# A two-block fp32 network on one core: attentions and scan rearranged, heads by pairs on halves of the array

## The chip, the cores and the metric

The kernel runs on one core of a Trainium2 chip. The metric is the device time of one execution in microseconds (us); the time before is the median of three runs, 975.42 us (974.31 to 978.83). Engines: PE is TensorE (matmuls), DVE is VectorE, ACT is ScalarE, POOL is GpSimd, SP issues the weight transfers.

## The reference

One sequence of 256 rows with D = 1024 goes through two blocks, all in fp32. What the change touches:

```
h = rmsnorm(x);  aq, ak, av, hq, hf_fwd, hf_bwd, hi, hg = split(h @ w_in)
att = attention(rope(norm(aq)), rope(norm(ak)), av)   # 8 heads of 64, 2 kv heads
rec = gated scan over the sequence, both directions, 4 heads of 128
x += rmsnorm(concat(att, rec) @ w_out)
m = rmsnorm(mem);  k, v = split(m @ w_xkv)
x += rmsnorm(attention(rmsnorm(x) @ w_xq, k, v) @ w_xo)   # 4 heads of 256
x += rmsnorm(conv_ffn(rmsnorm(x), w_up, w_down))          # D_FF 2816
# second block
oa = differential attention (8 heads, two maps of 64 each), subnormed
ob = latent attention (8 heads, 128 + 64 wide, block-causal)
x += rms_norm((sig(ga) * (oa @ w_proj_a) + sig(gb) * (ob @ w_proj_b)) @ w_o)
x += rms_norm(gated ffn)
```

## The kernel before, in words

**Products.** Each fp32 product is made of three fp32r products: high x high, low x high, high x low (`products`, L545). Weights stream through `sb_ring`, two slots of 2 MB, in the order of `chunks`; each chunk is cut into pieces of 128x1024. For each piece ACT copies the high half (`ahead`, L1420, `whi`) and DVE subtracts it for the low half (L1944, `wlo`); four lows, those of `xkv2`, are made by POOL (`POOL_LO`, `split_lo`). A piece's halves live in one of three homes or, for the long streams, in lent buffers (`lent1` to `lent9`). `ahead(m)` on ACT and DVE means: make all halves up to piece m now; `ahead_of(name, n)`: up to the n-th piece of a chunk; `reached[...]` holds how far PE has come at a step.

**Order.** Every engine's order is the written order of its block; the engines meet in semaphores. PSUM banks 0 to 3 serve the streamed products (`next_g`), 4 to 7 (`M`) the attentions, turns and sums; `Banks` pairs "filled" with "emptied". `gemm_rows` makes 128-row outputs, `cols_half` transposed ones, `row_pass` one row block over two chunks of 512 columns.

**Scan.** `next_level(n)` on DVE: `ahead`, `double_keys(n-1)` (L2083), `double_queries(n-1)` (L2093), `keep_level(n)` (L2068, copies masked scores out of the banks). PE's scores of a level are L742. `rope1(r)` (L2138 to L2152) stands between levels on DVE: it turns row block r of q and k, then scales it by the rstd that POOL makes (L1289).

**Attention** (`attend` on PE, ACT and DVE). At step n: scores of head n into bank 4 or 5 (PE L853 for the first attention, 64 rows of the array, by head in the upper or the lower half); turning of the probs of head n-1 into bank 6 (L817); values of head n-2 into bank 7 (L841; 64 columns of the array for the first attention); then a fill, a piece or two of another product. DVE: recip and scaling of the probs of head n-1 (L2195, L2199), then max of head n (L2215), lows, then taking the values of n-2 (L1982, L1983). ACT: exp of head n (L1590), highs, copy of the turned probs of n-1 (L1606). The second attention (`attx`) has no fill. In the third (`mla`) a piece of `w_proj_a` is the fill, and `normalise_oa(1)` and `take_v(1)` are DVE's.

**Around.** `mem_norm_g` is turned by `turn_norm` (L692): matmuls with a diagonal of rstd as the moving side. `w_xo` comes in two chunks of 512 columns, each over all rows, through `row_pass`; `into_ffn` on ACT and DVE squares each half row as it fills (L1647, L2281), adds it (L2289), and makes the tiles of the next norm (L1665, L2307), which PE turned (`turn_norm_rows`, L642). In `ffn`, DVE and ACT make the gate's and the value's taps (L2394, L1744) between lows. ACT's order at the end of the third attention: two highs of `w_proj_b`, sigmoids of the gates (L1878), with highs between.

```
attend, DVE:  probs(n-1); max(n); ahead(+1); fill; take(n-2); ahead(+2)
attend, ACT:  exp(n);  ahead(+1); copy turned(n-1); fill;     ahead(+2)
```

Of the kernel before, what the change touches and what calls it, by code (L numbers as in the profile page):

```python
# [36 lines left out]
P = 128  # L37
S = 256
# [116 lines left out]
def build(nc, a, out):  # L155
    ctx = ExitStack()
    with ctx:
# [246 lines left out]
        for n in ("w_out", "w_xq", "w_xo"):  # L404
            for i in range(2):
                chunk(f"{n}{i}", a[n], KT, 512 * i, 512)
            if n == "w_out":
                chunk("xkv3", a["w_xkv"], KT, 512 * 3, 512)
# [39 lines left out]
        for name, _, k, n in chunks:  # L448
# [9 lines left out]
            elif name == "ukv":  # L458
                w = w.rearrange("p k (h d) -> p k h d", d=2 * P)
                for part in (0, P):  # L460
                    for i in range(2):
                        piece(name, w[:, :, 4 * i:4 * i + 4, part:part + P])
            else:
                step_k = PIECE // n
                for k0 in range(0, k, step_k):
                    piece(name, w[:, k0:min(k0 + step_k, k), :], k0)
# [42 lines left out]
        POOL_LO = ("xkv2",)  # L509
        lo_there, lo_counts = [], {"lo_dve": 0, "lo_pool": 0}  # L510
        for name, _, _ in pieces:
            which = "lo_pool" if name in POOL_LO else "lo_dve"
            lo_counts[which] += 1
            lo_there.append((which, lo_counts[which]))

        def lo_done(m):

            return s(lo_there[m][0]), lo_there[m][1]
# [16 lines left out]
        def _(pe):  # L535
# [47 lines left out]
            def gemm_rows(name, T, part=None, readers=1):  # L583
# [6 lines left out]
                for q in range(lo, end):  # L590
                    m, w = next_piece(name)
                    k0 = pieces[m][2]
                    if q == 0:
                        for key in keys:
                            banks.take(pe, key, next_g(), readers)
# [38 lines left out]

            def turn_rows(name, src, r, half, b, ready, readers):
# [22 lines left out]
            def cols_half(name, T, half, readers=1):  # L658

                key = f"{name}.{half}"  # L660
                for j in range(2):
                    m, w = next_piece(name)
                    if j == 0:
                        banks.take(pe, key, next_g(), readers)
# [30 lines left out]

            turn_norm("pre_mix_g", x)
# [5 lines left out]
            turn_norm("mem_norm_g", mem)  # L702
# [83 lines left out]
            def by_rows(scores, spans):  # L786

                def both(u, os):
                    for r in range(R):
                        mm = scores(u, os[0][:, r * S:r * S + spans[r]], r, spans[r])  # L790
                    return [mm]
                return both

            def attend(name, units, ready, scores, values, spans, fill=(), v_every=1, at_once=1):

                turned = [u for u in range(units) if (u + 1) % v_every == 0]
                for step in range(units + 2):
                    if step < units and step % at_once == 0:  # L800
                        if step == 0:
                            ready()
                        keys = [f"{name}.s{u}" for u in range(step, step + at_once)]
                        for u, key in enumerate(keys, step):
                            banks.take(pe, key, M[u % 2], R)
                        done = scores(step, [bank[banks.at[key][0]] for key in keys])
                        for key, mm in zip(keys, done):
                            mm.then_inc(banks.fill(key), 1)
                    if step >= 1 and step - 1 in turned:
                        u = step - 1  # L810
                        pe.wait_ge(s(f"{name}_probs"), turned.index(u) + 1)
# [9 lines left out]
                    if step >= 2 and step - 2 in turned:  # L821
                        u = step - 2
                        n = turned.index(u)
# [3 lines left out]
                        mm = values(u, bank[M[3]], probsT[:, n % 2, :])  # L827
                        mm.then_inc(banks.fill(key), 1)
                    if step < len(fill):
                        f, args = fill[step]  # L830
                        f(*args)
# [18 lines left out]
            def scores1(h, o, r, n):  # L850
                lo = (h % 2) * ATT_DIM
                kv = h // (ATT_HEADS // ATT_KV)
# [1805 lines left out]
```

## Time and profile before

| what | us |
|---|---|
| median of the runs | 975.42 |
| the profiled execution | 976.41 |
| its span | 974.6 |
| PE busy | 917.2 |
| DVE busy | 619.5 |
| ACT busy | 479.6 |
| POOL busy | 87.1 |
| granted clock, mean | 0.989 |

The span is the profiled time less what lies around it (1.8 us). PE is the engine with the most work; its idle time and the stretches in which its granted clock is below 1 are what the order can change.

### The profile page before, as it was taken

The numbers are of one execution on the slowest core, as the hardware profiler recorded it, in microseconds if no ns is written. First come the engines' busy times: TensorE is split into PE (matmuls) and PEld (weight loads), VectorE is DVE, ScalarE is ACT, GpSimd is POOL, SyncE is SP. The second block draws the span as 40 slices with busy tenths as digits, with TensorE's granted clock in tenths as the row PEclk, the third lists the DMA queues.
The fourth block names the chain that finished last, engine by engine and source line by source line (L and its number), as shares of the span: only waits on it lengthen the run. The fifth ranks groups of instructions, "written<-read, shape, count | busy, mean of one in ns | idle before, by whom it ended". The sixth has DMA issues, their size and how long they took to land.

```text
span 974.6 us, 13972 instructions
## 1 busy us (share of the span) xinstructions
PE 917.2 (94%) x5556; PEld 804.0 (82%) x5556; DVE 619.5 (64%) x973; ACT 479.6 (49%) x841; POOL 87.1 (9%) x122
## 2 busy tenths in 40 slices
PE   6999699799989999999999999999898999999997
PEld 5988597479867999989978878788676879999996
DVE  4767774556457857576876666667677684363654
ACT  5844244455436735454553446666445562342541
POOL 1210103000002000000013310002003010000000
PEclk9999799999999999999999999999999999999999
DMA  9434232254335634645543645434225584346451
GB/s 328 175 130 158 82 107 88 85 173 159 123 98 183 217 130 158 217 145 182 207 152 118 217 173 173 135 136 174 87 87 182 163 284 170 130 160 227 135 172 43
DMA packets 92720, 152.56 MB, mean 157 GB/s; under 512 B 1968, under 2 KB 52272, under 8 KB 92400
## 3 DMA queue, kind: packets, MB, share of 16 engines
q1 hardware_dynamic: 92256, 150.94, 45.0%
q8 instruction: 44, 0.72, 0.3%
q10 hardware_dynamic: 288, 0.47, 0.2%
q0 software_dynamic: 112, 0.26, 0.1%
q14 instruction: 20, 0.16, 0.1%
HBM read 150.61 MB, written 1.05 MB: 156 GB/s over the span
## 4 chain that ended last, share of the span: by engine, by line
PE 67%; DVE 13%; ACT 5%; issue 4%; DMA 1%; DVEq 0%; ACTq 0%; POOLq 0%; POOL 0%
PE ps L545 58%; DVE sb_wlo L1944 2%; PE ps L841 2%; ACT sb_whi L1420 2%; DVE sb_b L2394 1%; PE ps L817 1%; DMA sb_ring<-in_w_in 1%; DVE sb_probs L2199 1%; PE ps L642 1%; DVE lent9lo L1944 1%; PE ps L678 1%; DVE lent8lo L1944 1%; PE ps L1060 1%; ACT lent8hi L1420 1%; ACT sb_b L1744 0%
## 5 line engine op out<-in xcount | busy, mean ns | idle before, releaser
L1944 DVE TENSOR_TENSOR sb_wlo<-sb_ring,sb_whi 128x1024 fp32r<-128x1024 f32 (+2 forms) x165 | 196.9, 1212 | 134.6 <-ACT sb_whi L1420 133.9
L1420 ACT ACTIVATE sb_whi<-sb_ring 128x1024 fp32r<-128x1024 f32 (+2 forms) x169 | 172.2, 1041 | 104.6 <-PE ps L545 98.2
L545 PE MATMUL ps<-sb_whi,sb_tbhi 128*128 128x512 f32 (+2 forms) x296 | 116.4, 393 | 3.8 <-DVE sb_wlo L1944 2.3
L545 PE MATMUL ps<-sb_whi,sb_tblo 128*128 128x512 f32 (+2 forms) x296 | 113.4, 383 | 0.0
L545 PE MATMUL ps<-sb_wlo,sb_tbhi 128*128 128x512 f32 (+2 forms) x296 | 113.3, 383 | 0.0
L545 PE MATMUL ps<-sb_whi,sb_tahi 128*128 128x512 f32 (+1 forms) x180 | 70.5, 391 | 9.3 <-DVE sb_wlo L1944 9.0
L545 PEld LDWEIGHTS ps<-sb_whi,sb_tbhi 128*128 128x128 f32 x296 | 55.6, 188 | 16.1 <-DVE sb_wlo L1944 3.6
L545 PE MATMUL ps<-sb_wlo,sb_tahi 128*128 128x512 f32 (+1 forms) x180 | 68.1, 378 | 0.0
L545 PE MATMUL ps<-sb_whi,sb_talo 128*128 128x512 f32 (+1 forms) x180 | 68.1, 378 | 0.0
L545 PEld LDWEIGHTS ps<-sb_whi,sb_tblo 128*128 128x128 f32 x296 | 55.6, 188 | 10.8
L545 PEld LDWEIGHTS ps<-sb_wlo,sb_tbhi 128*128 128x128 f32 x296 | 55.7, 188 | 9.2
L545 PE MATMUL ps<-sb_tahi,sb_whi 128*128 128x256 f32 x216 | 61.8, 286 | 0.6 <-DVE sb_b L2443 0.4
L545 PE MATMUL ps<-sb_talo,sb_whi 128*128 128x256 f32 x216 | 61.1, 283 | 0.0
L545 PE MATMUL ps<-sb_tahi,sb_wlo 128*128 128x256 f32 x216 | 61.1, 283 | 0.0
L545 PE MATMUL ps<-sb_tbhi,sb_whi 128*128 128x256 f32 x208 | 59.8, 287 | 0.0
L1744 ACT ACTIVATE sb_b<-ps,sb_col 128x256 f32<-128x256 f32 x44 | 22.2, 561 | 76.0 <-PE ps L545 76.0
L545 PE MATMUL ps<-sb_tblo,sb_whi 128*128 128x256 f32 x208 | 59.4, 285 | 0.0
L545 PE MATMUL ps<-sb_tbhi,sb_wlo 128*128 128x256 f32 x208 | 59.3, 285 | 0.0
L1903 ACT ACTIVATE sb_b<-ps 128x512 f32<-128x512 f32 x11 | 6.6, 597 | 91.5 <-PE ps L545 91.5
L545 PEld LDWEIGHTS ps<-sb_whi,sb_tahi 128*128 128x128 f32 x180 | 34.4, 191 | 17.8 <-DVE sb_wlo L1944 11.3
L1306 POOL TENSOR_TENSOR sb_st<-sb_st 128x1 f32<-128x1 f32 x14 | 4.1, 292 | 491.4 <-ACT sb_probs L1647 491.4
L1590 ACT ACTIVATE sb_probs<-ps,sb_st 128x256 f32<-128x256 f32 (+1 forms) x40 | 17.8, 449 | 52.8 <-DVE sb_st L2215 29.0
(364 smaller groups left out, 2428.8 us busy)
## 6 DMA issues: line engine op xcount, KB each, us to landing
sb_ring<-in_w_in SPq DMA_DIRECT2D x15, 2048.0 KB, 7.9
sb_ring<-in_w_up SPq DMA_DIRECT2D x22, 1024.0 KB, 5.2
sb_ring<-in_w_down SPq DMA_DIRECT2D x11, 1024.0 KB, 7.2
sb_ring<-in_w_ffn_gate SPq DMA_DIRECT2D x11, 1024.0 KB, 5.3
sb_ring<-in_w_ffn_up SPq DMA_DIRECT2D x11, 1024.0 KB, 5.9
sb_ring<-in_w_ffn_down SPq DMA_DIRECT2D x11, 1024.0 KB, 8.4
sb_ring<-in_w_xkv SPq DMA_DIRECT2D x4, 2048.0 KB, 8.0
sb_ring<-in_w_out SPq DMA_DIRECT2D x2, 2048.0 KB, 7.8
```

The lines of the kernel that those rows point to most:

```text
L545: mm = pe.matmul(o, l[a_], r[b_], start=(start and n == 0), stop=(stop and n == 2), skip_group_check=not check)
L642: mm = pe.transpose(bank[b][:, j * P:(j + 1) * P], src[:, r, k * P:(k + 1) * P], ident)
L678: mm = pe.transpose(bank[b][:, j * S + r * P:j * S + (r + 1) * P], src[:, r, k * P:(k + 1) * P], ident)
L817: mm = pe.transpose(bank[M[2]][:, kt * S + r * P:kt * S + (r + 1) * P], probs[:, u % 4, r * S + kt * P:r * S + (kt + 1) * P], ident)
L841: mm = pe.matmul(o[part:part + w, j * S + q0:(j + 1) * S], v[:, kt, c:c + w], pT[:, kt * S + q0:(kt + 1) * S], start=(kt == 0), stop=(kt = ...
L1060: pe.matmul(bank[M[i]][:, r * S:r * S + n], qaT[d, h, r * P:(r + 1) * P], kaT[d, h, 0:n], start=(r == 0), stop=False, skip_group_check=True)
L1420: act.activation(piece_pair(m)[0], src, ACT.Copy).then_inc(s("hi_done"), 1)
L1590: act.activation(probs[:, u % 4, r * S:r * S + spans[r]], bank[b][:, r * S:r * S + spans[r]], ACT.Exp, bias=smax[name][:, R * u + r:R * u ...
L1744: act.activation(conv[g][:, 2 * j + c, :], bank[banks.at[key][0]][:, c * S:(c + 1) * S], ACT.Identity, bias=COL[:, COL_CONVB + at:COL_CONV ...
L1944: dve.tensor_tensor(low, pieces[m][1], high.bitcast(F32), ALU.subtract).then_inc(s("lo_dve"), 1)
L2199: i = dve.tensor_scalar(p[r], p[r], d[:, r:r + 1], None, ALU.mult)
L2394: dve.scalar_tensor_tensor(dst, src, COL[:, at:at + 1], dst, ALU.mult, ALU.add).then_inc(banks.release(key) if last and c else s("ffn1_tap ...
```

## The change

- **First attention by pairs of heads.** The scores of two heads alternate between the row halves of the array, into banks 4 and 5; their probs are turned into banks 6 and 7; the values of the two alternate between column halves, into one bank. Pieces of `xkv1` and `xkv2` stand between, `rec` is turned before the last values. On DVE the maxima of both heads, a low, the probs of both, one taking per pair.
- **`attend` for the others.** On DVE max and probs of head n are in one step, with the wait for ACT's exp between them; on PE fills stand at "scored", "turned" or "valued".
- **Second attention.** `w_xq1` and pass 0 of `w_xo` are its fills. `w_xo` is cut by contraction rows into chunks of 4 x 1024, so that each piece needs one 128-row block of the attention's output, and both column halves of a row block fill at the end of the pass.
- **Scan.** `double_keys(n)` stands right behind `keep_level(n)`; `rope1` is split into `rope1_turn` and `rope1_scale`; a low comes ahead of the first turn.
- **Small ones.** `mem` is scaled by DVE and turned by plain transposes (`turn_scaled`); POOL makes no lows; `xkv3` goes into banks 6 and 7; in the first ffn both lows (and highs) of a down part come before the gate; all highs of `w_proj_b` come before the sigmoids; `turn_oa(1)` comes one step later in the third attention.

```diff
-        POOL_LO = ("xkv2",)
...
+        for i in range(2):
+            chunk(f"w_xo{i}", a["w_xo"][512 * i:512 * (i + 1), :], KT // 2, 0, D)
...
+            def scores1(p):
+                keys = [f"att1.s{2 * p + i}" for i in range(2)]
+                for i, key in enumerate(keys):
+                    banks.take(pe, key, M[i], R)
+                done = [None, None]
+                for r in range(R):
+                    for i in range(2):
+                        d = slice(i * ATT_DIM, (i + 1) * ATT_DIM)
+                        done[i] = pe.matmul(bank[M[i]][:, r * S:(r + 1) * S], qT1[d, p, r * P:(r + 1) * P],
+                                            kT1[d, p // 2, :], start=True, stop=True)
...
+            def values1(p):
...
+                for kt in range(2):
+                    for i in range(2):
+                        d = slice(i * ATT_DIM, (i + 1) * ATT_DIM)
+                        mm = pe.matmul(bank[M[2]][d, 0:S], qkv[:, kt, at:at + ATT_DIM],
+                                       probsT[:, i, kt * S:(kt + 1) * S], start=(kt == 0), stop=(kt == 1),
+                                       skip_group_check=True)
...
-            gemm_rows("xkv3", memT)
+            gemm_rows("xkv3", memT, into=M[2:])
...
+            attend("attx", X_HEADS, readyx, by_rows(scoresx, (S, S)), valuesx, (S, S),
+                   {(0, "scored"): [(cols_half, "w_xq1", hTx, 0, (0,))], (1, "scored"): [(cols_half, "w_xq1", hTx, 0, (1,))],
+                    (1, "turned"): [(cols_half, "w_xq1", hTx, 1, (0,))], (2, "turned"): [(cols_half, "w_xq1", hTx, 1, (1,))],
+                    (3, "valued"): [(xo_of, 0)], (4, "valued"): [(xo_of, 1)], (5, "valued"): [(xo_of, 2), (xo_of, 3)]})
...
@@ ACT, into_ffn
-                ahead_of(q1, 3)
+                ahead_of(q1, 4)
                 post_rows_of(post, f"{q0}.0", 0, 0)
-                ahead_of(q1, 4)
...
@@ ACT and DVE, ffn
+                    if i >= 2:
+                        ahead_of(f"f{f}.d{i - 1}", 2)
                     gate(i, i % 2)
-                        ahead_of(f"f{f}.d{i - 1}", 2)
...
@@ ACT, behind the third attention
-            ahead_of("w_proj_b_20", 4)
+            ahead_of("w_proj_b_21", 4)
             for r in range(R):
-                for i, gate in enumerate((siga, sigb)):
+                for gate in (siga, sigb):
                     act.activation(gate[:, r, :], gate[:, r, :], ACT.Sigmoid).then_inc(s("gates"), 1)
-                    if i == 0:
-                        ahead_of("w_proj_b_21", 2 * r + 2)
...
@@ DVE, scan
             def next_level(n):
-                if 0 < n < LEVELS:
-                    double_keys(n - 1)
                 ahead(reached[f"level{n}"] + 1)
                 if 0 < n < LEVELS:
                     double_queries(n - 1)
                 keep_level(n)
+                if n < LEVELS - 1:
+                    double_keys(n)
...
-            rope1(0)
+            ahead(reached["level5"] + 2)
+            rope1_turn(0)
             next_level(6)
-            rope1(1)
+            rope1_scale(0)
+            rope1_turn(1)
             next_level(7)
+            rope1_scale(1)
...
@@ DVE, third attention
-                   fill=[(normalise_oa, (1,)), (take_v, (1,)), (oaT_lo, (1,)), (lambda: None, ()), (lambda: None, ()),
...
+                   {0: [(take_v, 1), (normalise_oa, 1)], 2: [(oaT_lo, 1)], 5: [(take_a, 0, 0)], 6: [(take_a, 0, 1)],
```

**PE, first attention, one step late in it.** `sb_b2` holds the rotated q and k, `sb_b1` the values, `sb_probs` the probs. Before, a step of one head (there is no fill left at this place):

```order
L853 MATMUL ps4<-sb_b2 128x256 [waits emptied4]
L853 MATMUL ps4<-sb_b2 128x256
L817 MATMUL ps6<-sb_col,sb_probs 128x128 [waits emptied6,att1_probs]
L817 MATMUL ps6<-sb_col,sb_probs 128x128 x3
L841 MATMUL ps7<-sb_probsT,sb_b1 64x256 [waits emptied7,emptied6]
L841 MATMUL ps7<-sb_probsT,sb_b1 64x256
```

And now, the last pair; between the turns and the values stand twelve matmuls of `xkv2` (L541), of which the first is shown:

```order
L884 MATMUL ps4<-sb_b2 128x256 [waits emptied5,emptied4]
L884 MATMUL ps5<-sb_b2 128x256
L884 MATMUL ps4<-sb_b2 128x256
L884 MATMUL ps5<-sb_b2 128x256
L896 MATMUL ps6<-sb_col,sb_probs 128x128 [waits emptied6,att1_probs]
L896 MATMUL ps6<-sb_col,sb_probs 128x128 x3
L896 MATMUL ps7<-sb_col,sb_probs 128x128 [waits emptied7,att1_probs]
L896 MATMUL ps7<-sb_col,sb_probs 128x128 x3
L541 MATMUL ps0<-sb_whi,sb_tbhi 128x512 [waits lo_done]
...
L910 MATMUL ps6<-sb_probsT,sb_b1 64x256 [waits emptied6,emptied7]
L910 MATMUL ps6<-sb_probsT,sb_b1 64x256 x3
```

Two heads share one round of turns and values, with a piece between the turns and the values that read them.

**DVE, behind scan level 5.** `sb_b6` holds the decayed keys, `sb_b1` q and k, `sb_st` the rstd. Before:

```order
L2068 COPY_PREDICATED sb_b9<-sb_masks,ps5 128x512 [waits emptied5,filled5]
L2124 TENSOR_REDUCE sb_st<-sb_b0 128x10 [waits qk1_squares] x2
L2138 TENSOR_TENSOR sb_b0<-sb_b1,sb_tsq 128x512 [waits qk1_sq]
...
L2145 TENSOR_TENSOR sb_b1<-sb_b1,sb_b0 128x320
L2149 TENSOR_TENSOR sb_b1<-sb_b1,sb_st 128x512 [waits qk1_rstd,dve_step]
L2152 TENSOR_TENSOR sb_b1<-sb_b1,sb_st 128x128 x2
L2083 TENSOR_TENSOR sb_b6<-sb_b6,sb_b8 128x16x32 [waits totals,scan_k,scan_keys]
L2083 TENSOR_TENSOR sb_b6<-sb_b6,sb_b8 128x16x32 [waits totals]
L1944 TENSOR_TENSOR sb_wlo<-sb_ring,sb_whi 128x1024 [waits hi_done] x2
```

And now:

```order
L2161 COPY_PREDICATED sb_b9<-sb_masks,ps5 128x512 [waits emptied5,filled5]
L2176 TENSOR_TENSOR sb_b6<-sb_b6,sb_b8 128x16x32 [waits totals,scan_k,scan_keys]
L2176 TENSOR_TENSOR sb_b6<-sb_b6,sb_b8 128x16x32 [waits totals]
L2217 TENSOR_REDUCE sb_st<-sb_b0 128x10 [waits qk1_squares] x2
L2033 TENSOR_TENSOR sb_wlo<-sb_ring,sb_whi 128x1024 [waits hi_done]
L2231 TENSOR_TENSOR sb_b0<-sb_b1,sb_tsq 128x512 [waits qk1_sq]
...
L2238 TENSOR_TENSOR sb_b1<-sb_b1,sb_b0 128x320
L2033 TENSOR_TENSOR sb_wlo<-sb_ring,sb_whi 128x1024 [waits hi_done]
```

The keys moved ahead of the rope, one low ahead of it and one behind, and the scaling with `qk1_rstd` behind level 6.

## Rows read from the trace of the kernel before

**Rows 1.** Page of the profile, part 1, engines: busy us, share, count

```profile
PE 917.2 (94%) x5556; PEld 804.0 (82%) x5556; DVE 619.5 (64%) x973; ACT 479.6 (49%) x841; POOL 87.1 (9%) x122
```

**Rows 2.** Table of stretches, columns as in its head line, first attention

```profile
141.68:195.65 53.97, 47.06 (x249) 35.24 (x249) 28.43 (x58) 24.09 (x55) 11.40 (x6) 0.97 0.22 78
```

**Rows 3.** Waits of PE, 141 to 219 us: total, times, longest

```profile
PE ps L817 <- DVE sb_probs L2199: 5.9, 5, 2.0
PE ps L841 <- DVE sb_talo L1983: 1.1, 1, 1.1
PE ps L545 <- DVE sb_b L2252: 1.0, 1, 1.0
```

**Rows 4.** Waits of PE, 230 to 330 us

```profile
PE ps L817 <- DVE sb_probs L2199: 3.7, 3, 2.2
PE ps L841 <- DVE sb_talo L1983: 1.6, 1, 1.6
PE ps L892 <- ACT sb_b L1499: 1.1, 1, 1.1
```

**Rows 5.** Waits of PE, 676 to 745.5 us

```profile
PE ps L817 <- DVE sb_probs L2199: 4.6, 3, 1.8
PE ps L545 <- DVE lent8lo L1944: 0.9, 1, 0.9
```

**Rows 6.** Timeline of PE at the scan: start, duration, engine, line; idle before

```profile
115.87 0.79 PE L545 MATMUL ps<-sb_whi,sb_tahi 128*128 128x512 f32 x1 [7.79 <-DVE sb_wlo L1944]
121.14 1.05 PE L742 MATMUL ps<-sb_b 128*128 128x128 f32 x8
```

**Rows 7.** Table of stretches behind two gaps; PEclk follows POOL

```profile
110.90:121.10 10.20, 5.23 (x12) 4.13 (x13) 7.96 (x15) 3.99 (x5) 0.00 (x0) 0.50 0.38 130
151.80:155.20 3.40, 3.39 (x16) 3.39 (x17) 1.34 (x4) 2.81 (x7) 0.77 (x1) 0.51 0.85 268
```

**Rows 8.** Instructions of line L1060, durations in ns, forms last

```profile
L1060 PE MATMUL ps<-sb_b x64: 272/374/378, 594.4 to 660.5; 64*128 64x128 f32 x32, 64*128 64x256 f32 x32
```

**Rows 9.** Timeline of PE at the first head of that attention

```profile
594.44 0.93 PE L1060 MATMUL ps<-sb_b 64*128 64x128 f32 x8
595.20 0.22 PE L1040 MATMUL ps<-sb_maskrows 64*128 64x128 bf16 x2
```

**Rows 10.** Timeline of PE at whole-array scores of the third attention

```profile
681.46 0.39 PE L1201 MATMUL ps<-sb_b 128*128 128x128 f32 x2
681.68 0.60 PE L1199 MATMUL ps<-sb_b 128*128 128x256 f32 x2
682.12 0.59 PE L1201 MATMUL ps<-sb_b 128*128 128x256 f32 x2
```

**Rows 11.** Timeline of DVE at the scan

```profile
110.08 0.69 DVE L2149 TENSOR_TENSOR sb_b<-sb_b,sb_st 128x512 f32<-128x512 f32 x1 [2.34 <-POOL sb_st L1289]
111.09 1.28 DVE L2083 TENSOR_TENSOR sb_b<-sb_b 128x512 f32<-128x512 f32 x2
114.59 1.22 DVE L1944 TENSOR_TENSOR sb_wlo<-sb_ring,sb_whi 128x1024 fp32r<-128x1024 f32 x1 [2.21 <-ACT sb_whi L1420]
```

**Rows 12.** Timeline of PE at the first attention, two places

```profile
141.68 1.13 PE L853 MATMUL ps<-sb_b 64*128 64x256 f32 x4
142.74 0.39 PE L545 MATMUL ps<-sb_tbhi,sb_whi 128*128 128x256 f32 x1
...
161.33 1.08 PE L841 MATMUL ps<-sb_probsT,sb_b 128*64 128x256 f32 x4
```

**Rows 13.** Timeline at the end of pass 0 of w_xo, ACT and PE

```profile
293.88 0.58 ACT L1647 ACTIVATE sb_probs<-ps 128x512 f32<-128x512 f32 x1
...
300.31 0.66 PE L642 MATMUL ps<-sb_col,sb_b 128*128 128x128 f32 x4
```

**Rows 14.** Timeline of PE in the first ffn, one of eight such gaps

```profile
365.30 0.47 PE L545 MATMUL ps<-lent8hi,sb_tahi 128*128 128x512 f32 x1 [0.31 <-DVE lent9lo L1944]
```

**Rows 15.** Timeline of ACT at w_proj_b

```profile
729.42 1.28 ACT L1878 ACT_TABLE_LOAD   x1
```

More of the change, by code:

```diff
@@ L593, in gemm_rows @@
                     if q == 0:
-                        for key in keys:
-                            banks.take(pe, key, next_g(), readers)
+                        for r, key in enumerate(keys):
+                            banks.take(pe, key, into[r] if into else next_g())
                     for r, key in enumerate(keys):
@@ L633, in row_pass, with xo_piece, xo_pass @@
                             piece_used(m, mm, key if q == count - 1 else None)
+            def xo_piece(k, r, held):
+                if r == 0:
+                    held.append(next_piece(f"w_xo{k // 4}"))
+                m, w = held[k]
+                keys = [f"w_xo{c}.{r}" for c in range(2)]
+                if k == 0:
+                    for key in keys:
+                        banks.take(pe, key, next_g())
+                tile_there(k, r)
+                for c, key in enumerate(keys):
+                    mm = products(bank[banks.at[key][0]][:, :], [t[:, k, r * P:(r + 1) * P] for t in oxT],
+                                  [t[:, 0, c * 512:(c + 1) * 512] for t in w], k == 0, k == KT - 1)
+                    if k == KT - 1:
+                        mm.then_inc(banks.fill(key), 1)
+                if r == R - 1:
+                    piece_used(m, mm, keys[1] if k == KT - 1 else None)
+            def xo_pass(r, held, then, first=0):
+                for k in range(first, KT):
+                    if k in then:
+                        then[k]()
+                    xo_piece(k, r, held)
             def turn_rows(name, src, r, half, b, ready, readers):
@@ new lines, in turn_probs1 @@
+            def turn_probs1(p):
+                for u in (2 * p, 2 * p + 1):
+                    pe.wait_ge(s("att1_probs"), u + 1)
+                    b = M[2 + u % 2]
+                    banks.take(pe, f"att1.t{u}", b)
+                    for kt in range(2):
+                        for r in range(R):
+                            mm = pe.transpose(bank[b][:, kt * S + r * P:kt * S + (r + 1) * P],
+                                              probs[:, u % 4, r * S + kt * P:r * S + (kt + 1) * P], ident)
+                    mm.then_inc(banks.fill(f"att1.t{u}"), 1)
@@ L1574, in square_oa, with attend @@
                                    accum_out=stats["oa"][0][:, at:at + 1]).then_inc(s("oa_sq"), 1)
[L1576 to L1577 removed]
+            def attend(name, units, spans, fill):
                 for step in range(units + 1):
@@ new lines, in take_att1 @@
+            def take_att1(p):
+                key = f"att1.o{p}"
+                split_out(*(t[:, p, :] for t in mixT), psum(key, S)).then_inc(banks.release(key), 1)
+            first1 = pieces_of["xkv1"][0]
+            for p in range(ATT_HEADS // 2):
+                max1(p)
+                ahead(first1 + 2 * p + 3)
+                probs1(p)
+                if p == 0:
+                    finish_rec()
+                else:
+                    take_att1(p - 1)
+                ahead(first1 + 2 * p + 4)
```

356 lines of the change are left out of this document (188 added, 168 removed).

## The prediction, made before the changed kernel ran

> **What bounds the kernel now.** I read the head of the profile first [rows 1]: TensorE (PE) is busy for 917.2 of 974.6 us, so the end is PE's chain, and the time is PE's work plus its idle gaps plus what a lowered clock adds. Then the table of stretches: of the first attention's 53.97 us PE works 47.06 [rows 2]. Then who PE waits for, at the three attentions that the change touches [rows 3 to 5]: VectorE (DVE), for `probs` (L817 <- L2199), for low halves of weights and of outputs, never for long for a transfer. Last the timelines at the gaps.
>
> Two prices. PE's clock: in the stretch behind the scan's 7.79 us of idleness the granted clock is 0.50 for 10.2 us, and behind a gap of 2.01 us it is 0.51 for 3.4 us [rows 3, 6, 7], the 1.2 GHz level in place of 2.4; a gap of 1.81 us before L817 [rows 5] was followed by no such stretch. A short drop thus costs 3.4 us at half pace, 1.7 us of work. And one shape on halves of the array: two matmuls with 64 rows each, started alternately on both row halves, are in the trace at L1060 [rows 8, 9]: eight records a head, four of N=128 and four of N=256, with 0.76 us from the first to the next line's start. One after the other they would take 2x0.22 + 2x0.44 = 1.32 us by the starts of whole-array matmuls [rows 10]. So the row halves of this array do run together.
>
> **The sum, part by part** (against the profiled execution, 976.41 us with a span of 974.6; the median of the three runs, 975.42, is 1.0 below it).
>
> *mem_norm.* 32 fp32 matmuls become 16 transposes, 1.9 us less on PE. But `hq` behind them waits for the lows of its pieces, which come from the same DVE, now with two 128x1024 scalings more. I take 0; bounds 0 and 1.9.
>
> *Scan, levels 6 to 8.* PE stands 7.79 us at 115.87, and then runs twelve matmuls in 5.3 us to level 7 at 121.14 [rows 6] because the clock is low. DVE's timeline shows why [rows 11]: after `keep_level(5)` come the key sums and the rope of row 0, with a wait of 2.34 us for POOL's rstd, and only then the keys of level 6 (L2083, at 111.09), on which ACT's gathering and highs hang, and the lows at 114.59. Now `double_keys(5)` stands right behind the keep, a low goes ahead of the rope, and the wait for rstd lies behind level 6. With these durations DVE's row is: keep ends 103.8, keys 105.1, key sums 106.5, low 107.8, rope 110.4, low 111.6, queries 112.9, keep 114.2. PE starts its piece at about 111.6 (a gap near 3), level 7 at 113.6, waits about 2.3 us once more for a low near 120.4, and level 8 comes at 129.2 in place of 134.44: **5.2 us**. The floor is 3.5 (a drop of the clock not hidden by the second wait), the ceiling 10.5 (the whole stall and what it cost in clock).
>
> *First attention.* Four terms, from level 8 to the first matmul of `w_out`. (a) Gaps: five waits of L817 for the probs, 5.9 us, and one of L841 of 1.05, together 6.9 us [rows 3]. Before, a head's probs came one step later on DVE, behind a whole 5.7 us of pieces and a low; now max, exp and probs of both heads of a pair are done while PE has a piece, and there is a piece between the turn and the values too. Walking the pairs, every wait is covered; behind `values(3)` the two turns of `rec` cover the copies. (b) The clock drop of 1.7. (c) Scores: eight heads at 1.06 us from start to start [rows 12], 8.5 us; as row halves in pairs half of that, **4.2**. (d) Values: eight at 1.01 us [rows 12], in alternate *column* halves of one bank. No row shows two column halves at work together. Bounds: 0, and 4.0 if as good as the rows; nearest row is L1060, a different direction, so I take the middle, 2.0. Together 6.9 + 1.7 + 4.2 + 2.0 = 14.8, **14.7** after the first turn moved. Four lows of `xkv2` come from POOL to DVE, 4 x 1.2 = 4.8 us, but takes become four of 0.85 instead of eight, 3.4 less, so DVE stays at 30 us in some 39 [rows 2].
>
> The Trainium skill, page "TensorE: Matmul & The Clock Gate", Part 3 (Packing small matmuls), measures column packing of three tiles at 2.38 times; by it the values would gain nearly 4 and the sum 2 more. No run here shows it.
>
> *xkv3.* Its sums go into banks that no residual holds; the gap of 1.04 at 218.72 [rows 3] goes: **1.0**.
>
> *Second attention.* PE waits 1.1 before the scores (L892), 3.7 before the turned probs (L817, the longest 2.2) and 1.6 before the last values (L841), 6.4 us [rows 4], and the 2.2 brings a drop of 3.4 us. There is no fill in the loop now; the change puts the four pieces of `w_xq1` and pass 0 of `w_xo` (re-cut by contraction rows, so that a head's output is used as soon as it is there) between the steps. With 1.4 to 2.9 us of fill in each step against DVE's chain of max 0.68, exp 1.3, recip and probs 0.8, all is hidden: 6.4 + 1.7 = **8.1**; floor 4, if the last steps still wait.
>
> *Into the first ffn: a loss.* Because `w_xo` is now cut by contraction, both column halves of a row fill only at the end of their pass. Before, the first was squared and residual-multiplied in the middle (293.88 in [rows 13]). At the end of pass 0 ACT and DVE have everything at once; PE turns the normed row 0 after 8.2 us of pass 1 (300.31 in [rows 13]) without a wait, and the chain now takes 10.1: 1.9 lost. At the end of pass 1 it is worse: ACT's row is square of `w_xo0.1`, then `tiles_hi(0,.)`, so the high tiles of row 0, which the next pass needs, wait for the end of pass 1 and then take 0.8 + 1.2 and DVE's low another 1.1. That is 2.7 lost. Sum **-4.6**; bounds -3 and -8 (a drop of the clock, and its echo).
>
> *First ffn.* `ahead_of(d,2)` before the gate: eight gaps of 0.3, of which one is shown [rows 14], where the low of the second down piece came late, go: **2.4**. The taps then come 1.2 us later and PE does not wait for them for another iteration. Floor 1.
>
> *Third attention and w_proj_b.* Two things. Before the sigmoids ACT had done only some of `w_proj_b`'s highs [rows 15], with the table load of 1.28 and the sigmoids between them; PE then waits 0.9 + 0.6 + 0.6 + 0.6 = 2.7 us for lows [rows 5]. All five highs now come first, and ACT is done with them when PE is at the first; the gates come 4 us later, the POOL products at 1.9 each after them, and the merge still before PE needs it. In the loop, gaps 1.81, 1.58, 1.17 and 0.50 (L817's three, and one more) [rows 5] go in part: the probs come in their own step, but `take_v(1)` and `normalise_oa(1)` stand ahead of the low of the second piece, so PE waits 3.2 us there instead of 2.3, with a drop; then 1.5. Net of it all **1.5**; bounds -1.5 and 5.
>
> Unchanged: 9.4 us at the start and all gaps of 500 to 670 and of the second ffn.
>
> Sum: 0 + 5.2 + 14.7 + 1.0 + 8.1 - 4.6 + 2.4 + 1.5 = 28.3 us. 976.4 - 28.3 = 948.1, against the median 1.0 less: **947 us**.
>
> **The rivals.**
> *Column halves don't overlap* (or wholly do). Values gain 0 or 4 instead of 2: 949 or 945. Nothing in the trace speaks either way, since L841 with 128x64 is always followed by another kind of work. Chance 0.25 and 0.25 within the forecast's own case.
> *The covers are too thin.* My walk hides every wait at the attentions, and DVE's in-step wait for ACT's exp puts the low for PE's next piece behind it. If each of the 4 + 4 steps shows 0.7 us and one clock drop stays at each attention, 5.6 + 3.4 = 9 us come back: 956. For: L817 was the line that waited most [rows 3 to 5]. Chance 0.2. The Trainium skill, page "TensorEngine Tiling (Array Packing)", PSUM Bottleneck, says the same as a rule: packing speeds up TensorE but not the emptying of PSUM.
> *The scan's stall vanishes and mla's order is right:* 5 more at the scan, 3 more at mla: 939. Chance 0.1.
> *Halves don't run as said.* If the alternation gave nothing at all (both heads' matmuls in turn), only (c) and (d) fall out: 953. Speaks against: the starts at L1060 [rows 8, 9]. Chance 0.05.
> *Slower than before: the low clock lasts.* If the gap at the scan (3 us) drops the clock and the half-used array of the pairs with short waits between keeps it at 1.2 GHz up to `w_out`, the first attention's 39 us of PE work take 39 us more: 947 + 39 = 986. It decides once the clock stays low over more than 28 us of PE's work. For: it stayed low for 10.2 us at the scan [rows 7]. Against: it came back after 3.4 us at 151.8 though PE stood still again and again behind it [rows 3]. Chance 0.03.
>
> **How the numbers follow.** 0.62 for the forecast (943 to 951), 0.2 for 956, 0.1 for 939, 0.05 for 953, 0.03 for 986. The range that leaves out 2 in 10 goes from 938 to 959: it takes in mla's and the ffn entry's bad ends. About 5 us (0.5%) is what a measurement of this kernel tells from no change. Faster by that: 0.95; within: 0.02; slower: 0.03.
>
> **What would show it.** Level 8 near 129 and `w_out` near 176; no L-line of the turned probs waiting over 0.5 us in either attention; scores of a pair in 1.06 us; values of a pair between 1.0 and 2.0; ffn gaps of 0.3 gone; a new wait of about 2 us before the first turn of the normed rows and of over 2 at the end of pass 1; a wait of 3 near the second piece of the third attention. I am wrong if the granted clock shows long stretches at 0.5, or if PE's gaps before 330 sum to more than 12 us beside the 9.4 at the start.

## The result, and the profile after

The changed kernel takes 931.95 us (median of 4 runs, 931.06 to 932.55) against 976.1 (4 runs) of the kernel before on the same chip: ratio 0.9545, 95% interval [0.952, 0.9569]. It was forecast to be faster; the size was not, 947 with a range down to 938. The profiled executions' spans are 974.6 and 929.3, 45.3 us apart, and PE's idle time fell from 51.3 to 26.4 us, the start's 9.4 and 9.2 included.

The head of the page, which answers to [rows 1]:

```profile
span 929.3 us, 13932 instructions
PE 896.8 (97%) x5540; PEld 794.2 (85%) x5540; DVE 616.0 (66%) x969; ACT 479.0 (52%) x841; POOL 79.9 (9%) x118
```

PE has 20 us less busy time. Of it 8.2 are the halves (eight heads' scores and values in the time of four), 1.9 mem_norm, 1.4 the start (below). The rest, 9 us, is put down to the low clock and to the modelled ends of matmuls before a gap, which count as busy (estimates of about 4 us each: half of the PE work in the low stretches, and 0.16 us for each of 23 gaps fewer). PE's waits, in the stretches that answer to [rows 3], [rows 4] (with the entry of the ffn) and [rows 5] (total, times, longest):

```profile
PE ps L541 <- DVE sb_wlo L2033: 0.6, 1, 0.6
...
PE ps L541 <- DVE sb_tblo L2413: 1.6, 1, 1.6
PE ps L663 <- DVE sb_b L2404: 1.2, 2, 0.7
PE ps L541 <- DVE sb_wlo L2033: 0.8, 1, 0.8
PE ps L541 <- DVE lent8lo L2033: 0.4, 1, 0.4
...
PE ps L844 <- DVE sb_probs L2305: 1.3, 1, 1.3
PE ps L866 <- DVE sb_talo L2076: 1.0, 1, 1.0
```

Neither the first nor the second attention waits for probs any more. The 0.6 us of the first line stand at 196.82, in `xkv3`; what is left between 217 and 300 us lies at the entry of the ffn.

The scan, answering to [rows 6] and [rows 11]. First PE, then DVE:

```profile
99.92 2.02 PE L769 MATMUL ps<-sb_b 128*128 128x128 f32 x16
101.70 0.48 PE L541 MATMUL ps<-sb_whi,sb_tahi 128*128 128x512 f32 x1
...
109.82 2.44 PE L769 MATMUL ps<-sb_b 128*128 128x128 f32 x16 [2.38 <-DVE sb_b L2161]
111.91 0.56 PE L541 MATMUL ps<-sb_tbhi,sb_whi 128*128 128x256 f32 x1
```

```profile
102.93 1.21 DVE L2033 TENSOR_TENSOR sb_wlo<-sb_ring,sb_whi 128x1024 fp32r<-128x1024 f32 x1
106.62 1.21 DVE L2033 TENSOR_TENSOR sb_wlo<-sb_ring,sb_whi 128x1024 fp32r<-128x1024 f32 x1
107.76 1.28 DVE L2186 TENSOR_TENSOR sb_b<-sb_b 128x512 f32<-128x512 f32 x2
108.97 1.32 DVE L2161 COPY_PREDICATED sb_b<-sb_masks,ps 128x512 f32<-128x512 int32 x2
110.18 1.27 DVE L2176 TENSOR_TENSOR sb_b<-sb_b 128x512 f32<-128x512 f32 x2
```

PE goes straight on behind level 6 (101.70) with two pieces: the stall of 7.79 us is gone whole. What is left is 2.38 us before level 7, for DVE's `keep` at 108.97 and the queries at 107.76. The clock falls behind it (granted 0.50, the 1.2 GHz level, from 111.3 to 114.7):

```profile
111.30:114.70 3.40, 3.40 (x18) 3.40 (x18) 3.37 (x10) 0.00 (x0) 0.00 (x0) 0.50 0.02 7
```

The first attention, answering to [rows 12]: the scores of one pair and, further on, the values of one.

```profile
132.16 1.14 PE L884 MATMUL ps<-sb_b 64*128 64x256 f32 x8
133.23 0.39 PE L541 MATMUL ps<-sb_tbhi,sb_whi 128*128 128x256 f32 x1
...
161.90 1.08 PE L910 MATMUL ps<-sb_probsT,sb_b 128*64 128x256 f32 x8
162.91 0.50 PE L541 MATMUL ps<-sb_whi,sb_tbhi 128*128 128x512 f32 x1
```

Both now hold eight records, two heads, in 1.07 and 1.01 us; one head took 1.06 and 1.01 [rows 12]. Point by point, the same place in both traces (start on PE; "the norm's turn" is the first turn of the norm behind `w_out`):

| from, to | before | after | gain | forecast |
|---|---|---|---|---|
| start to first scan level | 55.71 | 52.32 | 3.4 | 0 |
| level 0 to level 6 | 47.60 | 47.60 | 0.0 | 0 |
| level 6 to level 8 | 31.13 | 25.01 | 6.1 | 5.2 |
| level 8 to `w_out` | 61.21 | 43.83 | 17.4 | 14.7 |
| `w_out` to the norm's turn | 34.08 | 33.64 | 0.4 | 1.0 |
| that to the turn of row 0 (second attention, pass 0) | 70.58 | 62.27 | 8.3 | 6.2 |
| that to the ffn's start | 28.79 | 31.10 | -2.3 | -2.7 |
| first ffn | 169.58 | 164.96 | 4.6 | 2.4 |
| to the third attention's scores | 178.11 | 177.96 | 0.2 | 0 |
| third attention and `w_proj_b` | 68.49 | 61.25 | 7.2 | 1.5 |
| to the end | 229.32 | 229.36 | 0.0 | 0 |

### The profile page after: what moved, and what is told of

It is laid out like the page before. It is cut to its first block, busy times and chain, and to the rows that moved or that the text cites. A ratio compares the mean times of both kernels' runs of the same rounds, so it can differ in the third digit from the quotient of the medians.

```text
span 929.3 us, 13932 instructions
## 1 busy us (share of the span) xinstructions
PE 896.8 (97%) x5540; PEld 794.2 (85%) x5540; DVE 616.0 (66%) x969; ACT 479.0 (52%) x841; POOL 79.9 (9%) x118
## 3 DMA queue, kind: packets, MB, share of 16 engines
HBM read 150.61 MB, written 1.05 MB: 163 GB/s over the span
## 4 chain that ended last, share of the span: by engine, by line
PE 81%; DVE 9%; ACT 4%; issue 3%; DMA 2%; POOL 0%; DVEq 0%; POOLq 0%; SPq 0%; ACTq 0%
PE ps L541 71%; DVE sb_wlo L2033 2%; DMA sb_ring<-in_w_in 2%; ACT sb_whi L1485 1%; PE ps L866 1%; PE ps L713 1%; PE ps L699 1%; PE ps L663 1%; PE ps L962 1%; PE ps L769 1%; PE ps L1137 1%; DMA sb_x<-in_x 1%; DVE sb_b L2186 1%; ACT sb_probs L1737 0%; DVE sb_b L2161 0%
## 5 line engine op out<-in xcount | busy, mean ns | idle before, releaser
L2033 DVE TENSOR_TENSOR sb_wlo<-sb_ring,sb_whi 128x1024 fp32r<-128x1024 f32 (+2 forms) x169 | 201.8, 1210 | 108.6 <-ACT sb_whi L1485 108.1
L541 PE MATMUL ps<-sb_whi,sb_tbhi 128*128 128x512 f32 (+2 forms) x296 | 116.7, 394 | 2.8 <-DVE sb_wlo L2033 2.8
L541 PE MATMUL ps<-sb_whi,sb_tblo 128*128 128x512 f32 (+2 forms) x296 | 113.5, 383 | 0.0
L541 PE MATMUL ps<-sb_wlo,sb_tbhi 128*128 128x512 f32 (+2 forms) x296 | 113.5, 383 | 0.0
L541 PE MATMUL ps<-sb_whi,sb_tahi 128*128 128x512 f32 (+1 forms) x180 | 69.4, 386 | 0.7 <-DVE sb_wlo L2033 0.6
L541 PEld LDWEIGHTS ps<-sb_whi,sb_tbhi 128*128 128x128 f32 x296 | 55.7, 188 | 14.9 <-DVE sb_wlo L2033 4.6
L541 PE MATMUL ps<-sb_wlo,sb_tahi 128*128 128x512 f32 (+1 forms) x180 | 67.3, 374 | 0.0
L541 PE MATMUL ps<-sb_whi,sb_talo 128*128 128x512 f32 (+1 forms) x180 | 67.2, 374 | 0.0
L541 PEld LDWEIGHTS ps<-sb_whi,sb_tblo 128*128 128x128 f32 x296 | 55.6, 188 | 10.7
L541 PEld LDWEIGHTS ps<-sb_wlo,sb_tbhi 128*128 128x128 f32 x296 | 55.7, 188 | 9.2
L2499 DVE SCALAR_TENSOR_TENSOR sb_b<-ps,sb_col,sb_b 128x255 f32<-128x255 f32 x88 | 36.1, 475 | 40.8 <-ACT sb_b L1837 40.8
L541 PE MATMUL ps<-sb_tahi,sb_whi 128*128 128x256 f32 x216 | 61.8, 286 | 0.6 <-DVE sb_b L2548 0.3
L541 PE MATMUL ps<-sb_talo,sb_whi 128*128 128x256 f32 x216 | 61.2, 283 | 0.0
L541 PE MATMUL ps<-sb_tahi,sb_wlo 128*128 128x256 f32 x216 | 61.1, 283 | 0.0
L541 PE MATMUL ps<-sb_tbhi,sb_whi 128*128 128x256 f32 x208 | 60.6, 291 | 0.0
L541 PE MATMUL ps<-sb_tblo,sb_whi 128*128 128x256 f32 x208 | 59.4, 286 | 0.0
L541 PE MATMUL ps<-sb_tbhi,sb_wlo 128*128 128x256 f32 x208 | 59.4, 286 | 0.0
L541 PEld LDWEIGHTS ps<-sb_tahi,sb_whi 128*128 128x128 f32 x216 | 41.4, 192 | 1.4 <-issue 0.7
```

The source lines that it names most:

```text
L541: mm = pe.matmul(o, l[a_], r[b_], start=(start and n == 0), stop=(stop and n == 2), skip_group_check=not check)
L2033: dve.tensor_tensor(low, pieces[m][1], high.bitcast(F32), ALU.subtract).then_inc(s("lo_done"), 1)
L2499: dve.scalar_tensor_tensor(dst, src, COL[:, at:at + 1], dst, ALU.mult, ALU.add).then_inc(banks.release(key) if last and c else s("ffn1_tap ...
```

## The experiments

Each is an edit of the changed kernel; the time of it to set beside is 932.0. They were timed in four sets, in each beside the kernel before and none beside the changed kernel itself. The kernel before had medians of 974.3 to 976.3 in the four sets, and the start alone differs by up to 1.4 us between profiles (below). A difference of medians of about 1.5 us or less is therefore no proof by itself; the same stretch in both traces is the finer measure, and is given where it matters.

**Values, order within a pair.**

```diff
-                for kt in range(2):
-                    for i in range(2):
+                for i in range(2):
+                    for kt in range(2):
```

> Only the order of four matmuls changes: the values of a pair no longer alternate between the column halves, both halves of the contraction of one head come first, then those of the other. Theory of the prediction (columns overlap by half): four pairs go from about 1.5 to 2.0 us, 2 us in all. Rival (columns overlap wholly, as the changed kernel's trace seems to say with eight records in 1.01 us from start to start): 4 pairs times 1.01, so +4.0 us, about 936. If instead the order of issue does not matter, 0.

Measured 931.85 (931.66 to 932.7). The values of a pair still take 1.02 us from start to start:

```profile
162.48 1.09 PE L910 MATMUL ps<-sb_probsT,sb_b 128*64 128x256 f32 x8
163.50 0.50 PE L541 MATMUL ps<-sb_whi,sb_tbhi 128*128 128x512 f32 x1
```

So it is the third case: the alternation is worth nothing. That left open what this time comes from, since in this order, too, two heads take the time of one.

**Scores, order within a pair.** The same edit of the loops over `r` and `i` in `scores1`.

> Only the order of the scores changes: both row blocks of one head, then those of the other, so that two matmuls in a row sit on the same row half. If row halves overlap only when the issue alternates, the pair takes 2.1 in place of 1.06 us, and the kernel +4.2 us. If the array takes up to two matmuls ahead by itself, the middle two of each pair would still overlap, and it costs about 3 us or less.

Measured 932.06 (931.48 to 932.93): also nothing. In both orders the eight records start in twos, 7 ns apart in the changed kernel and 14 ns here, with 0.3 us to the next two. The first two of this run:

```profile
133.09 0.49 PE L884 MATMUL ps<-sb_b 64*128 64x256 f32 x2
```

A single head's four records stand one behind the other (next experiment), so each two are one of either head: the second head's first matmul starts ahead of the first head's second, though it is written behind it. So here the order of writing did not decide when the second head started.

**Scores, with work between the heads.**

```diff
+                for i in range(2):
...
+                    if i == 0:
+                        turn_probs1(p - 1)
```

> The changed kernel with the turns of the pair before put between the scores of the two heads, in three of the four pairs; same instructions. The order within a pair was worth nothing. If two heads' scores overlap only because they are next to each other, each of the three pairs takes 1.06 us more: +3.2 us, about 935. If the array's halves overlap across other work too, 0.

Measured 935.94 (935.03 to 936.22), 4.0 more; from the wait before the q/k turns to that at `xkv3` it takes 72.6 us instead of 68.8. Of these 3.8 us, 3.2 are the three second heads; most of the rest lies in the turns, which take 1.03 us here instead of 0.87. One such pair:

```profile
160.64 1.13 PE L882 MATMUL ps<-sb_b 64*128 64x256 f32 x4
161.70 1.09 PE L909 MATMUL ps<-sb_col,sb_probs 128*128 128x128 f32 x8
162.73 1.13 PE L882 MATMUL ps<-sb_b 64*128 64x256 f32 x4
```

Four records of one head, the turns, four records of the other: each head has its 1.06 us to itself again. The overlap needs the two heads' matmuls next to each other, not alternation.

**Values, with a turn between the heads of the last pair.**

```diff
             turn_rec(0)
+            values1_apart(3, 0)
             turn_rec(1)
-            values1(3)
+            values1_apart(3, 1)
```

> The changed kernel with one of the two turns of rec put between the values of the last pair's two heads; same instructions. If column halves overlap only when the two heads stand next to each other, as the row halves of the scores do, the last pair's values take 1.0 us more, and w_out starts 1.0 us later. If they overlap by half, 0.5; if the saving has another cause, 0.

```profile
168.25 1.08 PE L910 MATMUL ps<-sb_probsT,sb_b 128*64 128x256 f32 x4
169.26 0.65 PE L699 MATMUL ps<-sb_col,sb_b 128*128 128x128 f32 x4
169.85 1.08 PE L910 MATMUL ps<-sb_probsT,sb_b 128*64 128x256 f32 x4
```

One head's two matmuls take 1.01 us from 168.25 to 169.26, as long as a pair of heads in the changed kernel. From the turns of the last probs to the first matmul of `w_out` it takes 4.00 us instead of 2.95: 1.05 more, as the theory of whole overlap says. The median, 933.32, is 1.4 above.

**mem_norm by the diagonal again** (`turn_norm` for `turn_scaled`, DVE makes the diagonal, POOL waits for the turned banks).

> The changed kernel with mem_norm turned by 32 matmuls with the diagonal again. Prediction's theory: the work behind it waits for DVE anyway, so 0 us. Rival: nothing behind it waits, and it costs the 1.9 us of TensorE's work in full: the first scan level starts at 54.2 in place of 52.3, about 933.9.

Measured 934.03 (933.4 to 934.23), 2.1 more. On PE:

```profile
38.29 3.74 PE L713 MATMUL ps<-sb_diag,sb_b 128*128 128x128 f32 x32
54.42 1.80 PE L769 MATMUL ps<-sb_b 128*128 128x128 f32 x14 [0.89 <-ACT sb_b L1550]
```

3.74 us of turns instead of 1.91, and the first level is that much later than at 52.32, with the same 0.89 us of wait before it. Nothing behind the turns waited, so my zero was wrong.

**The scan's order of before.** (ScalarE's gathering of the keys goes back with it.)

```diff
+                if 0 < n < LEVELS:
+                    double_keys(n - 1)
                 ahead(reached[f"level{n}"] + 1)
...
-                if n < LEVELS - 1:
-                    double_keys(n)
...
-            ahead(reached["level5"] + 2)
             rope1_turn(0)
+            rope1_scale(0)
             next_level(6)
...
```

> The changed kernel with the order of the scan's levels 6 to 8 as before (keys doubled at the start of the next level, the rope whole and ahead of them). If the order alone made the stall, TensorE waits 7 to 8 us before the second piece behind level 6 again and the kernel loses what the two traces differ by between level 6 and level 8, 6.1 us: about 938. Prediction's theory: 5.2. If the move of the other lows did part of it, less than 4.

Measured 938.95 (938.24 to 939.79), 7.0 more, of which 6.5 lie between levels 6 and 8 in the trace (31.50 instead of 25.01 us), and the stall is back to the digit:

```profile
113.02 0.80 PE L541 MATMUL ps<-sb_whi,sb_tahi 128*128 128x512 f32 x1 [7.79 <-DVE sb_wlo L2032]
```

**Queries and keep ahead of the rope.**

```diff
             ahead(reached["level5"] + 2)
+            double_queries(5)
+            keep_level(6)
+            double_keys(6)
+            ahead(reached["level6"] + 1)
             rope1_turn(0)
-            next_level(6)
             rope1_scale(0)
+            ahead(reached["level6"] + 2)
```

> Behind scan level 5 VectorE now does queries, keep and keys of level 6 ahead of the rope of row 0. Theory: TensorE's wait of 2.4 us before level 7 (L769 on the keep) and the wait of 1.5 us or the low clock behind it come from the rope and a low that stand ahead of the keep; both go, -2 to -4 us, about 929. Rival: the low half for the second piece behind level 7 comes later instead, and TensorE waits as long there: within 1 us.

Measured 930.8 (930.72 to 931.03), 1.2 less, and 1.6 less between levels 6 and 8 in the trace (23.38 instead of 25.01 us): between the theory and the rival. The wait of 2.4 us before level 7 is gone, but two waits for lows follow, 1.67 at 115.14 and 0.54 at 118.81. DVE's row is full here, 15.9 of the 16 us from 108 to 124.

**The two halves of the ffn edit.** DVE's and ScalarE's order moved back alone:

> The changed kernel with the first ffn's order of halves (and the second's) as before: eight idle gaps of TensorE of about 0.3 us come back. Theory of the prediction, that a gap costs what the trace calls idle: +2.4 us. Rival, that each stop costs its idle time plus the overlap of the pipelined end and a slower first matmul, 0.5 to 0.6 us from start to start: +4.5 us, about 936.5.

PE's side alone:

```diff
-                    if len(held_down[i]) == k:
-                        held_down[i].append(next_piece(f"f{f}.d{i}"))
...
-                    held_down[i] = []
+                    held_down[i] = [next_piece(f"f{f}.d{i}") for _ in range(2)]
```

> The changed kernel in which TensorE waits for both pieces of a down part before its first matmul, as before, while VectorE's and ScalarE's order stays new. Moving VectorE's and ScalarE's order back alone brought no gap back. Theory now: the gaps went because TensorE no longer waits for the second piece before it uses the first. If that alone did it, eight gaps of 0.3 come back, each 0.5 to 0.6 us from start to start: +4.5 us, about 936.4. If either side alone suffices (the lows come earlier now), no gap comes back and it costs 0.

And both together:

> The changed kernel with both halves of the ffn edit moved back: VectorE's and ScalarE's order, and TensorE's wait for both pieces of a down part. If either side alone is enough (each alone moved back brought none of the eight gaps), together they bring all eight back: +4.5 us from the first ffn's start to its end, 186.5 in place of 181.9, about 936.5. If the gain of the first ffn came from elsewhere, +0 to 0.7 as with each alone.

Measured 932.66, 933.37 (932.25 to 933.52) and 936.85 (936.65 to 937.4). With the first alone none of the gaps is in the trace, with the second alone one of 0.57 us near the end of the ffn, with both all eight (and a ninth of 0.2), of which the first:

```profile
332.15 0.28 PE L541 MATMUL ps<-sb_tbhi,lent3lo 128*128 128x256 f32 x1
332.74 0.47 PE L541 MATMUL ps<-lent8hi,sb_tahi 128*128 128x512 f32 x1 [0.31 <-DVE lent9lo L2030]
333.04 0.40 PE L541 MATMUL ps<-lent8lo,sb_tahi 128*128 128x512 f32 x1
```

Either side is enough; only moved back together do they bring the gaps back. And this is where the price of a gap shows. The nine add to 2.7 us in brackets (the idle time that the timeline prints), but the ffn (from the turn at its entry to the first wait behind it) takes 186.5 us instead of 181.9. From 332.15 to 332.74 are 0.59 us where the pitch is 0.12, and the next start is 0.30 instead of 0.23 later: 0.54 us lost, of which the bracket says 0.31. The bracket counts from the modelled end of a matmul, and that lies 0.16 us behind the point at which the next could have started.

**The sigmoids between the highs again** (the edit of the diff, undone).

> The changed kernel with the sigmoids of the gates between the high halves of w_proj_b again. Prediction's theory: four idle gaps of 0.9 + 3 x 0.6 come back, +2.7 us. Rival, that a gap costs more than its idle time: +3.9 us, about 935.8. If the merge was what bounded, 0.

Measured 936.4 (936.24 to 936.71), 4.4 more, 3.8 in the trace of `w_proj_b`. The four gaps of [rows 5] come back, of which two:

```profile
694.20 0.50 PE L541 MATMUL ps<-lent8hi,sb_tahi 128*128 128x512 f32 x1 [0.93 <-DVE lent8lo L2035]
696.43 0.51 PE L541 MATMUL ps<-lent9hi,sb_tahi 128*128 128x512 f32 x1 [0.58 <-DVE lent9lo L2035]
```

**The probs of the third attention one step later.** On DVE, for that attention alone, `probs(n-1)` stands ahead of `max(n)`.

> In the third attention alone VectorE makes the probs of head n one step later, ahead of the maximum of head n+1, as before. Theory now: the probs in their own step are what took the waits of the turned probs away; the loop gets 2 to 4 us longer. Prediction's theory: the loop was bound by the low halves behind take and normalise, so the place of the probs is worth under 1 us.

Measured 937.94 (937.63 to 938.16), 6.0 more, above both of the values expected:

```profile
PE ps L844 <- DVE sb_probs L2294: 6.8, 3, 3.0
```

The place of the probs alone is worth more than the whole loop gained (3.4 us), since `take_v(1)` and the scaling of `oa` now stand ahead of them, too. About 1.3 us of it are the clock: behind the first of the three waits (2.6 us) it is granted at 0.50 for 3.4 us.

**The entry of the first ffn.**

```diff
                 ahead_of(in0, 4)
-                post_rows_of(post, f"{q0}.1", 0, 1)
+                if f == 2:
+                    post_rows_of(post, f"{q0}.1", 0, 1)
                 for half in range(2):
                     tiles_hi(norm, T, gain, 0, half)
+                if f == 1:
+                    post_rows_of(post, f"{q0}.1", 0, 1)
```

> At the entry of the first ffn ScalarE makes the high tiles of row block 0 ahead of the square of w_xo's second row block, which fills only at the end of pass 1. Theory of the prediction: that square holds the tiles back, and TensorE's wait of 1.59 us at the start of the next pass (270.14) goes, -1.6 to -2.4 us, about 930. Rival: the tiles' low halves on VectorE stand behind other work anyway, so the wait only moves: within 0.5 us.

Measured 929.23 (928.79 to 930.25), 2.7 less, 2.3 in the trace. The waits for `tblo` and `lent8lo` at the entry are gone:

```profile
PE ps L663 <- DVE sb_b L2407: 1.2, 2, 0.7
PE ps L541 <- DVE sb_wlo L2036: 0.8, 1, 0.8
```

**Three edits together:** this one, the scan's, and `normalise_oa(1)` one step later in the third attention.

> Three edits together: the high tiles ahead of the square at the entry of the first ffn (-2.7 alone), the scan order of the kernel beside it in this set, and the scaling of the second half of oa one step later in the third attention, ahead of which its low and maximum now stand (TensorE's wait of 1.27 us for the second head's probs goes). If they add up: 932.0 - 2.7 - 3 - 1.3 = 925. If they only move waits, no less than 929.

Measured 927.2 us (926.06 to 927.5), ratio to the kernel before 0.9503 [0.9483, 0.9523]; it is the fastest version of this study. It was expected at 925, with 3 us for the scan's part. Of the 4.8 us less than the changed kernel, 2.7 and 1.2 are the first two by their medians (2.2 and 1.6 in this trace), and 1.3 us fit the wait for the second head's probs (1.27 at 650.40), which its trace no longer has.

## Why the prediction was right and wrong

**Right:** the sign; that PE's chain is the time; that the gaps of the first two attentions, of `xkv3` and of the ffn and the stall of the scan would go, and those of the third attention in part; that the row halves run together; that the new cut of `w_xo` costs at the entry of the ffn, by the mechanism named (ScalarE's high tiles behind the square of a bank that fills late): 2.7 us forecast for that part, 2.7 by the medians and 2.3 by the trace when it is undone, and 2.3 net in the table. The rivals of a DVE-bound attention and of a lasting low clock did not happen: between the start and the last 3 us the granted clock is below 1 in one short stretch only.

**The sum.** The traces differ by 45.3 us where 28.3 were forecast. The 17.0 between them are 5.7 at the third attention and `w_proj_b`, 3.4 at the start, 2.7 at the first attention, 2.2 at the first ffn, 2.1 at the second attention, 0.9 at the scan and 0.4 at the entry and 0.2 elsewhere, less 0.6 at `xkv3`.

**Wrong: the third attention, 7.2 us for 1.5.** This is the step that took the time out of the range, and 7.2 lies outside its own bounds, -1.5 and 5. It reads "PE waits 3.2 us there instead of 2.3, with a drop". It took DVE's first low in the loop for that of PE's next piece. It is that of the one after:

```profile
638.36 1.21 DVE L2033 TENSOR_TENSOR sb_wlo<-sb_ring,sb_whi 128x1024 fp32r<-128x1024 f32 x1
645.65 1.29 DVE L2645 TENSOR_TENSOR sb_b<-sb_b,sb_st 128x512 f32<-128x512 f32 x2
646.87 1.22 DVE L2033 TENSOR_TENSOR sb_wlo<-sb_ring,sb_whi 128x1024 fp32r<-128x1024 f32 x1
...
644.49 0.50 PE L844 MATMUL ps<-sb_col,sb_probs 128*128 128x128 f32 x3
644.75 0.48 PE L541 MATMUL ps<-sb_whi,sb_tbhi 128*128 128x512 f32 x1
```

PE starts the second piece at 644.75 without a wait; its low was made at 638.36, ahead of the loop, and the one at 646.87 serves the third piece (DVE's lows and PE's first uses of a piece pair off one to one, 279 of each in the trace). In [rows 5]'s stretch the 0.50 us had not been a wait for a low either, but for a bank (L2561). What `take_v(1)` and the scaling do hold up are the probs of the second head, by 1.27 us and without a drop. PE's waits in the loop fell from 5.1 to 2.2 us, and with what each gap costs beyond its bracket the loop gained 3.4; `w_proj_b` gained 3.8 where its four brackets say 2.7.

**Wrong: the same count at the scan, and mem_norm.** At the scan the step "PE starts its piece at about 111.6" was off by one piece in the same way; the lows for the two pieces from 101.70 were there (102.93 is the later one's, done at 104.14 for the piece at 104.56). It did not fit its own sum either: twelve matmuls at the full clock's 0.23 us take 2.8, which puts level 7 at 114.4 and not at 113.6. The total came out near (5.2, measured 6.1) because level 7 is bound by DVE's keep, whose time was right (level 7 comes 9.9 us behind level 6, forecast 10.3), and because behind level 7 there is a second hold-up, as forecast, for a low: level 8 comes 15.1 us behind level 7 (forecast 15.6) instead of 13.3. In this profile it shows as low clock, in most others as a wait of 1.5 us at full clock; the drop thus cost nothing of its own. The old stall's low clock had also looked longer than it was for PE's work: of the 10.2 us at 0.50 [rows 7], which the prediction puts behind the stall, 5.0 lay in it. At mem_norm, "`hq` behind them waits for the lows of its pieces" was asserted without a row, and the 1.9 us of PE's work, its upper bound, are what it is worth.

**Wrong: the size of a gap.** Term (a) of the first attention and the terms of the second attention, the ffn and `w_proj_b` were summed from the brackets. Nine gaps of 2.7 us in all cost 4.6; a bracket of 0.58 at `w_proj_b` cost 0.86.

**Two more waits.** At the end of pass 0 of `w_xo` the prediction has 1.9 us lost; the wait before the first turn of the normed rows is 0.66 us (264.67), 0.8 from start to start. Why it is shorter was not looked for. At `xkv3` the wait of 1.04 us went, but one of 0.58 us for a low (196.82) came, so 0.4 were gained and not 1.0.

**The middle taken for the column halves** was 2.0; it is 4.0, the upper bound. The trace could not tell; the figure of the Trainium skill (page "TensorE: Matmul & The Clock Gate", Part 3), 2.38 times for three column tiles, points to this side: tile for tile it would be 1.6 times for two, an estimate of 3.0 us for the values. The measured factor here is 2 for two heads. Sorted by what PE starts, the 17.4 us of the first attention are 6.9 of idle brackets, 4.5 in the scores' matmuls, 4.0 in the values', 1.5 in the turns of the probs (3.4 us for 32 records instead of 4.9) and 0.5 in all others; the clock drop of before is spread over these.

**Not the change:** 1.4 us of the 3.4 at the start lie in the turns of `pre_mix`, which no edit touches. Over the 16 profiles of this study they take 5.3 to 6.7 us with the same code; the changed kernel's and `ffn_back`'s:

```profile
9.23 5.27 PE L713 MATMUL ps<-sb_diag,sb_x 128*128 128x128 f32 x32 [9.23 <-DVE sb_diag L2048]
...
9.31 6.72 PE L713 MATMUL ps<-sb_diag,sb_x 128*128 128x128 f32 x32 [9.31 <-DVE sb_diag L2047]
```

It is the clock. Their 32 matmuls start 0.21 us apart at first and 0.11 us apart from 12.3 us on in the one profile and from 15.4 us on in the other. The trace's record of the granted clock begins there, at the full level (12.27 and 15.39 us; for the time before it has no record, and the views print 1.00). In all 16 profiles the pace doubles within 0.1 us of that point, 3.0 to 6.1 us behind the first matmul. So the changed kernel's profile has the luckiest start of all, and of the 45.3 us between the two profiles 1.4 are luck.

**For the range:** the bounds of the terms left out that a gap costs more than its bracket, which touched four of them at once, and the third attention went beyond its own bound.

## What to carry to other kernels

When lows or other prepared operands stand in a helper's row, count which consumer each one belongs to from the start of the stream; one piece of lead decided here whether an order was forecast to cost 3 us or cost nothing. Price a gap from start to start, not by the idle time in brackets. And two matmuls that use half of the array each should stand next to each other; in which order is the same, and four or eight whole-array turns between them took the gain away.

## What the runs showed of the hardware that was not expected

- Two heads on different column halves (128x64 tiles of L910, both into one bank) take 1.01 us, as one does; two on row halves 1.07. The overlap was the same with the matmuls of one head written together (931.85 and 932.06 us against 931.95; the second head's first record still starts 14 ns behind the first head's first) and gone with eight records of turns between the heads (each head 1.06 us).
- A short gap cost 0.54 us where the trace says 0.31, another 0.86 where it says 0.58.
- A wait of 2.38 us at the scan brought the clock down in the changed kernel's profile (0.50 granted over 3.4 us). In nine of the twelve profiles with this wait it is followed by a wait of 1.5 us for a low half some 6 us later instead, and level 8 comes 15.1 us behind level 7 in either. In `mla_late` a wait of 2.62 us was followed by 3.4 us at 0.50, and one of 3.00 us fifteen microseconds later was not. So the length of the gap alone does not decide; what does was not settled.
- The first matmuls run at half pace for 3.0 to 6.1 us, from profile to profile, at a place where the views print a granted clock of 1.00.
